# A fused two-block transformer kernel: the first scale and shift computed in eight chunks of 128 features

## The chip, the cores and the metric

The kernel runs on one core of a Trainium2 chip, as one program. The metric is the device time of one execution in microseconds (us); lower is better. TensorE (PE) does the matmuls and the transposes, VectorE (DVE) and ScalarE (ACT) the elementwise work, GpSimd (POOL) a few small operations and the issue of some transfers, and SyncE (SP) issues most transfers. Each engine works through its own instructions strictly in program order; semaphores order the engines against each other.

## The reference, cut to what matters

Two transformer blocks follow each other on x, which has 256 rows (positions) and 1024 features, all in fp32. The change touches the beginning of the first block:

```python
cond = jax.nn.silu(c)
mod = cond @ w_ada[l] + b_ada[l]                 # 1024 x 6144 weight, one row
sh1, sc1, g1, sh2, sc2, g2 = jnp.split(mod, 6, axis=-1)
h = _modulate(x, ln1_g[l], sh1, sc1)             # rms(x, g) * (1 + sc1) + sh1
u = h @ w_in[l]                                  # fox q, k, v | gates | diff q, k, v
fq, fk, fv, fg, dq, dk, dv = jnp.split(u, splits, axis=-1)
...                                              # "fox" attention (8 heads), "diff" attention (4 heads)
x = x + g1[:, None, :] * (mixed @ w_out[l])
```

After that come a gated MLP and a whole second block. They are the same before and after the change.

## The kernel before, in words

**Work list.** A function `plan()` writes one list, ORDER, of steps such as ("piece", ...), ("split", i), ("ada", j), ("evac", T). Each engine walks the whole list and emits only its part of each step. So the order of ORDER is the program order on every engine, and nothing overtakes on an engine.

**Matmuls.** The product is made precise by splitting both operands in two: a weight slab in `raw` (fp32, as loaded) is rounded to `whi` on ACT (L1079) and the rest, raw minus whi, goes to `wlo` on DVE (L1289). This pair is the step `split`. The operand hT has a high and a low half too. One `piece` is one k step (128 features) of one output tile of 256 rows x 512 columns: six matmuls of 512 columns, on the lines L794 (hi x hi), L795 (hi x lo) and L796 (lo x hi), for two row blocks. Output tiles of the first block are fox0 (q), fox1 (k), fox2 (v), diff0, diff1, diff2.

**Buffers.** `raw` has five slots (RAW) and the stream of loads is STREAM: each load waits until the load five places before it has been used. `whi` and `wlo` have three slots (SPL). A split i therefore waits on ACT and on DVE for `gemm_done` to reach i - 2, that is until the last matmul of slab i - 3 is through.

**The start.** `ada` steps multiply w_ada by silu(c), held as 32 equal columns (`cond32`). The first eight of them (L847) make scale and shift of the first norm in two halves of 512 features. A `mod` step brings the result to columns (L868), `turn` steps transpose the normalised x (L904), DVE applies scale and shift (L1388), and `part` steps (L1124 on ACT, L1404 on DVE) split the result into the two halves of hT. Four pieces of fox0 follow with the next four ada steps between them, and then the second half in the same way.

**The way to the first scores.** When a fox tile is complete, `evac` copies it to `tok` (ACT, L1224), squares it to `sq` (ACT, L1229) and sums the squares by head (DVE, L1608). `unit` takes the inverse roots on POOL (L1679 and L1681) and scales tok on DVE (L1450). `heads` transposes q and k of two heads (PE L939) and splits them (ACT L1158 and L1160, DVE L1459 and L1462). `fgate`, `logf` and `cum` make the forget gates: 24 small matmuls (L748), then DVE (L1423, L1425), ACT (an Exp and a Ln with a table load between them), DVE (L1430 to L1436). `vectors`, `setup` and `relbias` prepare small constants on DVE (L1305 to L1329), and POOL issues six transfers for `relbias`. `scores` are the first attention products (L748). After ("scores", 1) the first piece of diff0 follows.

Of the kernel before, what the change touches and what calls it, by code (L numbers as in the profile page):

```python
# [34 lines left out]
P = 128  # L35
# [21 lines left out]
V_C, V_LN1, V_LN2, V_MIX, V_FFN, V_PLE, V_BS, V_QK, V_DN = 0, 8, 16, 24, 32, 40, 48, 56, 60  # L57
V_ALL = 61
# [18 lines left out]
def plan():  # L77
# [81 lines left out]
    def parts(kind, n, pairs):  # L159
# [22 lines left out]
    tail += insert(fill, *[(j, [ada[10 + j]]) for j in range(8)])  # L182
    order += attention(list(range(FOX_P + DIFF_P)), tail, ada[18:20] + [("grow", 0)])
# [79 lines left out]
STREAM = [it for it in ORDER if it[0] in ("split", "ada")]  # L263
# [55 lines left out]
def build(nc, A, out):  # L319

    ctx = ExitStack()
    with ctx:
# [23 lines left out]
        cond32 = sb("cond32", [P, KC, 32])  # L346
        lam = sb("lam", [P, 6])
# [16 lines left out]
        aff1 = sb("aff1", [P, 4, S], F32, gg)  # L364
# [1462 lines left out]
```

## Time and profile before

| | before |
|---|---|
| median of 3 runs | 846.1 us (844.94 to 847.69) |
| profiled execution, span | 845.9 us |
| PE busy | 799.9 us (95%) |
| DVE busy | 473.1 us (56%) |
| ACT busy | 396.7 us (47%) |
| POOL busy | 57.9 us (7%) |
| bytes moved by DMA | 157.87 MB, mean 187 GB/s |

The span runs from the first to the last instruction of the profiled execution; nothing else of that execution's time is shown, and the span stands 0.2 us beside the median. A busy share is the time in which an engine executes, divided by the span. PE is the engine whose work fills the span, so what counts is where it stands idle and where it runs slowly.

### The profile page before, as it was taken

The page shows a single profiled execution, that of the slowest core. Times are in us where ns is not written, and L with a number is a line of the kernel's source. Part 1 is how long each engine was busy: PE and PEld are TensorE (multiplying, and loading weights), DVE is VectorE, ACT ScalarE, POOL GpSimd, SP SyncE. Part 2 cuts the span into 40 slices and gives each one's busy share as a digit, 9 for nine tenths or more (in the row PEclk, how much of TensorE's full clock was granted, in tenths as well). Part 3 has the DMA queues.
Part 4 walks back from the last instruction along what each step waited for, and adds up shares of the span by engine and source line. Part 5 has one row for each costly group of instructions (what it writes and reads, how often), then busy time and mean ns, then how long its engine had stood idle before and what let it go on. Part 6 is the DMA issues. An engine that isn't in the chain of part 4 may idle for free.

```text
span 845.9 us, 10042 instructions
## 1 busy us (share of the span) xinstructions
PE 799.9 (95%) x3874; PEld 628.0 (74%) x3874; DVE 473.1 (56%) x604; ACT 396.7 (47%) x544; POOL 57.9 (7%) x70
## 2 busy tenths in 40 slices
PE   4797999988999999999999999999999999999995
PEld 0266776545788889788878888787888888888884
DVE  0455776556655555553686546556565665535354
ACT  2335665544534444343644347666555454334262
POOL 4013011000000000000252000000000000000001
PEclk9799999999999999999999999999999999999998
DMA  9985245778456537556749564333456465554511
GB/s 292 374 270 188 68 163 196 307 249 313 169 184 199 174 85 239 183 180 198 266 146 333 166 196 149 105 117 117 155 168 199 152 197 159 189 199 143 186 45 50
DMA packets 74128, 157.87 MB, mean 187 GB/s; under 512 B 4046, under 2 KB 6295, under 8 KB 72034
## 3 DMA queue, kind: packets, MB, share of 16 engines
q1 hardware_dynamic: 71072, 151.08, 53.2%
q0 software_dynamic: 1872, 6.11, 2.2%
q8 instruction: 31, 0.51, 0.2%
q10 hardware_dynamic: 1138, 0.06, 0.1%
q14 instruction: 15, 0.12, 0.0%
HBM read 156.16 MB, written 1.07 MB: 186 GB/s over the span
## 4 chain that ended last, share of the span: by engine, by line
PE 87%; ACT 4%; DVE 3%; issue 3%; DMA 2%; SPq 1%; POOL 1%; DVEq 0%; POOLq 0%; ACTq 0%
PE PS L794 25%; PE PS L796 24%; PE PS L795 24%; PE PS L748 3%; PE PS L904 3%; DMA raw<-in_w_ada 2%; PE PS L856 2%; PE PS L847 1%; PE PS L1007 1%; ACT whi L1079 1%; PE PS L977 1%; PE PS L939 1%; SPq L717 1%; DVE wlo L1289 1%; ACT sc L1168 0%
## 5 line engine op out<-in xcount | busy, mean ns | idle before, releaser
L1289 DVE TENSOR_TENSOR wlo<-raw,whi 128x2048 fp32r<-128x2048 f32 (+1 forms) x122 | 279.6, 2294 | 185.1 <-ACT whi L1079 161.0
L1079 ACT ACTIVATE whi<-raw 128x2048 fp32r<-128x2048 f32 (+1 forms) x122 | 226.8, 1859 | 169.7 <-PE PS L796 156.4
L794 PE MATMUL PS<-whi,hT 128*128 128x512 f32 (+1 forms) x704 | 278.3, 395 | 6.4 <-DVE hT L1404 5.9
L796 PE MATMUL PS<-whi,hT 128*128 128x512 f32 (+1 forms) x704 | 272.3, 387 | 0.0
L795 PE MATMUL PS<-wlo,hT 128*128 128x512 f32 (+1 forms) x704 | 271.8, 386 | 0.0
L794 PEld LDWEIGHTS PS<-whi,hT 128*128 128x128 f32 x704 | 132.9, 189 | 36.8 <-issue 8.0
L796 PEld LDWEIGHTS PS<-whi,hT 128*128 128x128 f32 x704 | 132.8, 189 | 27.3
L795 PEld LDWEIGHTS PS<-wlo,hT 128*128 128x128 f32 x704 | 133.1, 189 | 24.3
L794 PE MATMUL PS<-whi,hidT 128*128 128x512 f32 x216 | 86.2, 399 | 0.0
L796 PE MATMUL PS<-whi,hidT 128*128 128x512 f32 x216 | 85.3, 395 | 0.0
L795 PE MATMUL PS<-wlo,hidT 128*128 128x512 f32 x216 | 85.3, 395 | 0.0
L795 PEld LDWEIGHTS PS<-wlo,hidT 128*128 128x128 f32 x216 | 40.6, 188 | 9.8 <-issue 0.2
L796 PEld LDWEIGHTS PS<-whi,hidT 128*128 128x128 f32 x216 | 40.6, 188 | 9.8
L794 PEld LDWEIGHTS PS<-whi,hidT 128*128 128x128 f32 x216 | 40.6, 188 | 9.7 <-issue 0.2
L1168 ACT ACTIVATE sc<-sc,nmax 128x128 f32<-128x128 f32 x64 | 28.6, 449 | 34.6 <-DVE nmax L1501 34.2
L1724 POOL TENSOR_TENSOR nss<-nss 128x2 f32<-128x2 f32 x5 | 0.9, 190 | 589.4 <-ACT mod L1069 361.0
L1129 ACT ACTIVATE hidT<-PS 128x512 fp32r<-128x512 f32 x27 | 14.6, 597 | 43.3 <-PE PS L904 43.3
L748 PEld LDWEIGHTS PS<-kT,qT 128*128 128x128 f32 x192 | 24.6, 190 | 9.0 <-issue 4.4
L748 PE MATMUL PS<-kT,qT 128*128 128x128 f32 (+1 forms) x192 | 27.3, 281 | 3.9 <-DVE kT L1462 2.5
L1409 DVE SCALAR_TENSOR_TENSOR hidT<-PS,hidT 128x512 fp32r<-128x512 f32 x27 | 17.4, 686 | 22.6 <-ACT hidT L1129 22.6
L847 PE MATMUL PS<-raw,cond 128*32 128x512 f32 x64 | 21.6, 813 | 8.7 <-DMA raw<-in_w_ada 8.7
L847 PEld LDWEIGHTS PS<-raw,cond 128*32 128x32 f32 x64 | 3.8, 133 | 23.2 <-issue 14.6
(223 smaller groups left out, 663.7 us busy)
## 6 DMA issues: line engine op xcount, KB each, us to landing
raw<-in_w_in SPq DMA_DIRECT2D x40, 1024.0 KB, 5.3
raw<-in_w_ff SPq DMA_DIRECT2D x32, 1024.0 KB, 5.2
raw<-in_w_ada SPq DMA_DIRECT2D x16, 1024.0 KB, 6.6
raw<-in_w_gate SPq DMA_DIRECT2D x10, 1024.0 KB, 5.1
raw<-in_w_up SPq DMA_DIRECT2D x10, 1024.0 KB, 5.1
raw<-in_w_down SPq DMA_DIRECT2D x10, 1024.0 KB, 5.1
raw<-in_w_ada SPq DMA_DIRECT2D x16, 512.0 KB, 10.3
raw<-in_w_out SPq DMA_DIRECT2D x8, 1024.0 KB, 5.1
```

What stands on the lines that cost most here:

```text
L748: last = pe.matmul(out_ap, a, b, start=(n == 0), stop=(n == len(pairs) - 1))
L794: pe.matmul(o, ah, wh, start=(k == 0), stop=False)
L795: pe.matmul(o, ah, wl, start=False, stop=False)
L796: return pe.matmul(o, al, wh, start=False, stop=end)
L847: last = pe.matmul(PS[r:r + 32, 7 - half, :], cond32[:, 2 * k + c, :], raw[:, slot, (2 * c + j) * W:(2 * c + j + 1) * W], start=(k + c == ...
L856: last = pe.matmul(PS[32 * j:32 * j + 32, 7, :], cond32[:, k, :], raw[:, slot, j * W:(j + 1) * W], start=(k == 0), stop=(k == KC - 1))
L904: last = pe.transpose(PS[:, b, o:o + P], src[:, t, c * P:(c + 1) * P], ident)
L1079: act.activation(slab_view(whi, i % SPL, i), slab_view(raw, slot, i), ACT.Copy).then_inc(hi_made, 1)
L1129: act.activation(hi.rearrange("p c s -> p (c s)"), PS[:, b, :], ACT.Copy, scale=1.0 if gain is None else gain).then_inc(turn_hi, 1)
L1168: act.activation(sc[:, n, c0:c1], sc[:, n, c0:c1], ACT.Exp, bias=nmax[:, a, t:t + 1], scale=-1.0, accum_out=lsum[:, a, t:t + 1]).then_inc( ...
L1289: dve.tensor_tensor(slab_view(wlo, i % SPL, i), slab_view(raw, slot, i), whole(slab_view(whi, i % SPL, i)), ALU.subtract).then_inc(lo_made, 1)
L1409: dve.scalar_tensor_tensor(out=lo.rearrange("p c s -> p (c s)"), in0=PS[:, b, :], scalar=1.0 if gain is None else gain, in1=hi.rearrange(" ...
```

## The change

The first scale and shift no longer come in two halves of 512 features but in eight chunks of 128. For each chunk j the kernel loads 1 MB of w_ada (128 scale columns and 128 shift columns of all 1024 rows, in two transfers of 512 KB with runs of 512 bytes), multiplies it (`rows`), copies the row to SBUF on ACT, turns it into columns with two one-column matmuls (`col`), applies it to the transposed x (`xT`) and splits the result (`part0`). Then come the k step j of fox0 and the k step j of fox1, from one slab of w_in of 128 rows x 1024 columns (0.5 MB). x is the first transfer of SP; c, the identity, ln1_g and the two bias rows are issued by ACT. The order of ORDER changes down to ("scores", 1); behind it the steps are the same.

```diff
-    order += [("cond", 0), ("sums", (0, 0)), ("sums", (0, 1)), ("norm", 0)]
-    order += ada[:4] + [("mod", 0), *turns("norm", 0, (0, 1)), ("split", None), *parts("norm", 0, (0, 1))]
     fox = [tile("fox", n, KC, "h") for n in range(2)]
-    order += insert(slab(fox[0], "w_in", 0, 0), *[(1 + j, [ada[4 + j]]) for j in range(4)])
-    order += [("mod", 1), *turns("norm", 0, (2, 3)), ("split", None), *parts("norm", 0, (2, 3))]
-    order += slab(fox[1], "w_in", W, 0) + [("vectors", 0), ("setup", 0), ("relbias", 0)]
-    order += slab(fox[0], "w_in", 0, 4) + [("evac", fox[0])]
-    now = slab(fox[1], "w_in", W, 4) + [("evac", fox[1])] + whole("fox", 2, "w_in", 2 * W, "h")
-    order += insert(now, (2, [("unit", 0)]), (2, [("fgate", 0)]), (4, [("logf", 0)]), (6, [("unit", 1)]),
-                    (7, [("cum", 0)]), (9, [("heads", 0)]), (10, [("scores", 0), ("heads", 1)]))
+    def chunk(j):
+        return [("col", j), ("split", None), ("part0", j)]
+    order += [("cond", 0), ("chunk", 0), ("sums0", 0), ("norm", 0), ("rows", 0), ("xT", 0), *chunk(0)]
+    order += [("xT", 1), ("chunk", 1), ("rows", 1)]
+    for j in range(KC):
+        slabs.append(dict(weight="w_in", row=j * P, chunks=1, col=0, cols=2 * W))
+        pair = [("piece", dict(T=fox[n], k=j, slab=j, off=n * W, first=n == 0, last=n == 1)) for n in range(2)]
+        order += [pair[0]] + (chunk(j + 1) if j + 1 < KC else []) + [pair[1]]
+        if j + 2 < KC:
+            order += [("xT", j + 2), ("chunk", j + 2), ("rows", j + 2)]
+    order += [("evac", fox[0]), ("evac", fox[1]), ("vectors", 0), ("setup", 0), ("relbias", 0), ("fgate", 0)]
+    now = whole("fox", 2, "w_in", 2 * W, "h")
+    order += insert(now, (1, [("unit", 0)]), (2, [("logf", 0)]), (4, [("unit", 1)]), (6, [("cum", 0)]), (7, [("heads", 0)]))
...
+    order += [("scores", 0), ("heads", 1)]
     order += attention(list(range(FOX_P + DIFF_P)), tail, ada[18:20] + [("grow", 0)])
...
+                if it[0] == "chunk":
+                    dst = raw[:, n % RAW, :].rearrange("p (k a c) -> p k a c", k=KC, a=2)
+                    for a in range(2):
+                        c = a * D + it[1] * P
+                        sp.dma_start(dst[:, :, a, :], A["w_ada"][0, :, c:c + P].rearrange("(k p) c -> p k c", p=P)
+                                     ).then_inc(raw_in[n % RAW], 16)
...
+                elif kind == "rows":
...
+                    for k in range(KC):
+                        r = 32 * (k % 4)
+                        last = pe.matmul(PS[r:r + 32, b, 0:256], cond32[:, k, :], raw[:, slot, k * 256:(k + 1) * 256],
+                                         start=k < 4, stop=k >= 4)
...
+                elif kind == "col":
+                    b = chunk_bank(i)
+                    dve.wait_ge(col_ps, i + 1)
+                    dve.wait_ge(ab0_made, 1 + i)
+                    dve.tensor_scalar(AB[:, 1, i:i + 1], PS[:, b, S:S + 1], col[:, V_B1 + i:V_B1 + i + 1], None, ALU.add)
+                    dve.scalar_tensor_tensor(out=AB[:, 0, i:i + 1], in0=PS[:, b, S + 1:S + 2],
...
+                    dve.tensor_scalar(aff1[:, i % 2, :], PS[:, b, 0:S], AB[:, 0, i:i + 1], AB[:, 1, i:i + 1],
+                                      ALU.mult, ALU.add).then_inc(aff_made, 1)
```

On ACT, at the place where the operand of the first tiles is split, the program before reads as follows (raw and whi are the weight slab and its high half, hT and aff the operand's high half and its source, tok and sq belong to the evacuation; the brackets list the semaphores that an instruction waits for).

```order
L1113 ACTIVATE xn<-x,nrs 128x1024 [waits norm_rs]
L1079 ACTIVATE whi<-raw 128x2048 [waits raw_in4]
L1124 ACTIVATE hT<-aff 128x512 [waits turn_aff] x2
L1079 ACTIVATE whi<-raw 128x2048 [waits raw_in0] x2
L1124 ACTIVATE hT<-aff 128x512 [waits turn_aff,gemm_done] x2
L1079 ACTIVATE whi<-raw 128x2048 [waits gemm_done,raw_in1]
```

In the changed program ACT has this at the second and third chunk (mod is the copied row of a chunk; L1112, L1122 and L1126 are the lines of the weight split, the row copy and the operand split).

```order
L1126 ACTIVATE hT<-aff 128x256 [waits aff_made]
L1122 ACTIVATE mod<-PS 128x256 [waits col_ps,rows_ps]
L1112 ACTIVATE whi<-raw 128x1024 [waits gemm_done,raw_in1]
L1112 ACTIVATE whi<-raw 128x1024 [waits gemm_done,raw_in2]
L1126 ACTIVATE hT<-aff 128x256 [waits aff_made]
L1122 ACTIVATE mod<-PS 128x256 [waits col_ps,rows_ps]
```

A weight split that waits for `gemm_done` now stands directly ahead of every operand split from the third slab on, and DVE has its halves of both in the same order.

On DVE, the program before has the constants, the fox sums and the gate in this order (hss are the sums of squares, wfgs the gate's weights, relrow the relative bias row, fgt the gate).

```order
L1289 TENSOR_TENSOR wlo<-raw,whi 128x2048 [waits gemm_done,hi_made,raw_in1]
L1305 COPY col<-PS 128x45 [waits vec_ps]
...
L1325 TENSOR_TENSOR wfgs<-wfg,wfgs 128x64 [waits wfg_hi,gate_w_in]
L1329 COPY relrow<-PS 16x384 [waits rel_ps]
L1289 TENSOR_TENSOR wlo<-raw,whi 128x2048 [waits gemm_done,hi_made,raw_in2]
L1608 TENSOR_REDUCE hss<-sq 128x16 [waits sq_in]
L1289 TENSOR_TENSOR wlo<-raw,whi 128x2048 [waits gemm_done,hi_made,raw_in3]
L1423 TENSOR_SCALAR fgt<-PS,bf 8x256 [waits fg_ps]
```

In the changed program the same steps stand on DVE like this (L1336 is the weight split, L1669 the sums, L1484 the gate).

```order
L1669 TENSOR_REDUCE hss<-sq 128x16 [waits sq_in] x2
L1380 COPY col<-PS 128x45 [waits vec_ps]
...
L1400 TENSOR_TENSOR wfgs<-wfg,wfgs 128x64 [waits wfg_hi,gate_w_in]
L1404 COPY relrow<-PS 16x384 [waits rel_ps]
L1484 TENSOR_SCALAR fgt<-PS,bf 8x256 [waits fg_ps]
L1486 SCALAR_TENSOR_TENSOR fgt<-fgt 8x256 [waits fg_abs]
L1336 TENSOR_TENSOR wlo<-raw,whi 128x2048 [waits gemm_done,hi_made,raw_in3]
```

Both sums now stand ahead of the constants, and the constants directly ahead of the gate.

## Rows read from the trace of the kernel before

**Rows 1.** The page: the span and the busy time of PE
```profile
span 845.9 us, 10042 instructions
PE 799.9 (95%) x3874; PEld 628.0 (74%) x3874; DVE 473.1 (56%) x604; ACT 396.7 (47%) x544; POOL 57.9 (7%) x70
```

**Rows 2.** Timeline of PE, start: start us, us, engine, line, what, idle before
```profile
9.10 3.63 PE L847 MATMUL PS<-raw,cond 128*32 128x512 f32 x8 [4.96 <-DMA raw<-in_w_ada]
...
32.17 0.76 PE L794 MATMUL PS<-whi,hT 128*128 128x512 f32 x1 [4.45 <-DVE hT L1404]
...
39.92 1.91 PE L847 MATMUL PS<-raw,cond 128*32 128x512 f32 x8
```

**Rows 3.** Timeline: the last unit, heads 0, scores 0, scores 1, first diff0 piece
```profile
80.72 1.23 DVE L1450 TENSOR_TENSOR tok<-tok,hrs 128x1024 f32<-128x1024 f32 x1 [0.38 <-POOL hrs L1681]
...
82.10 0.80 PE L939 MATMUL PS<-con,tok 128*128 128x128 f32 x4 [4.83 <-DVE tok L1450]
...
86.03 0.55 PE L748 MATMUL PS<-kT,qT 128*128 128x128 f32 x3 [0.58 <-DVE kT L1462]
...
94.49 0.55 PE L748 MATMUL PS<-kT,qT 128*128 128x128 f32 x3 [1.36 <-DVE kT L1462]
...
96.90 0.39 PE L794 MATMUL PS<-whi,hT 128*128 128x512 f32 x1
```

**Rows 4.** Groups by form: weight splits; busy us, mean ns, idle before
```profile
L1079 ACT ACTIVATE whi<-raw 128x2048 fp32r<-128x2048 f32 x114 | 218.3, 1915 | 147.1 <-PE PS L796 133.8 <-DMA raw<-in_w_in 13.0
L1289 DVE TENSOR_TENSOR wlo<-raw,whi 128x1024 fp32r<-128x1024 f32 x8 | 9.8, 1224 | 14.2 <-ACT whi L1079 14.1
L1079 ACT ACTIVATE whi<-raw 128x1024 fp32r<-128x1024 f32 x8 | 8.5, 1061 | 22.6 <-PE PS L796 22.6
```

**Rows 5.** Timeline of PE: first matmuls of two pieces, four pieces apart
```profile
57.39 0.50 PE L794 MATMUL PS<-whi,hT 128*128 128x512 f32 x1
...
62.98 0.39 PE L794 MATMUL PS<-whi,hT 128*128 128x512 f32 x1
```

**Rows 6.** A stretch (last columns: granted clock, DMA share, GB/s), and one issue row
```profile
413.00:414.00 1.00, 1.00 (x6) 0.84 (x5) 1.00 (x4) 0.39 (x1) 0.00 (x0) 1.00 1.00 344
...
ws<-in_w_sgu_spatial POOLq DMA_DIRECT2D x1, 512.0 KB, 5.1
```

**Rows 7.** A stretch, same columns: behind the idle time ahead of 32.17
```profile
32.00:38.00 6.00, 5.83 (x14) 2.38 (x14) 2.83 (x3) 0.00 (x0) 0.00 (x0) 0.50 1.05 381
```

**Rows 8.** Timeline: evacuation of fox0, constants, and the gate's matmuls
```profile
58.06 0.21 DVE L1305 COPY col<-PS 128x45 f32<-128x45 f32 x1
...
59.68 0.23 DVE L1325 TENSOR_TENSOR wfgs<-wfg,wfgs 128x64 fp32r<-128x64 f32 x1
...
63.18 1.03 ACT L1224 ACTIVATE tok<-PS 128x1024 f32<-128x1024 f32 x1 [1.79 <-PE PS L796]
...
65.16 1.22 DVE L1608 TENSOR_REDUCE hss<-sq 128x16 f32<-128x1024 f32 x1 [1.39 <-ACT sq L1229]
...
65.70 2.92 PE L748 MATMUL PS<-hT,wfgs 128*8 128x256 f32 x24
```

**Rows 9.** Timeline of POOL: first transfer of relbias, and one inverse root
```profile
60.66 0.59 POOL L1706 DMA_DIRECT2D skew_dram<-relrow  x1 [40.07 <-DVE relrow L1329]
...
66.77 2.94 POOL L1681 TENSOR_TENSOR hrs<-hrs,expo 128x16 f32<-128x16 f32 x1
```

**Rows 10.** Timeline of DVE and ACT: the gate, heads 0, a split
```profile
69.65 0.47 DVE L1423 TENSOR_SCALAR fgt<-PS,bf 8x256 f32<-8x256 f32 x1
...
72.78 0.41 DVE L1430 SCALAR_TENSOR_TENSOR fgt<-fgt 8x256 f32<-8x256 f32 x1 [1.08 <-ACT fgt L1142]
...
74.39 0.41 DVE L1436 SCALAR_TENSOR_TENSOR ncum<-fgt,ncum 8x256 fp32r<-8x256 f32 x1 [0.48 <-ACT ncum L1147]
...
82.93 0.96 ACT L1158 ACTIVATE qT<-PS,col 64x256 fp32r<-64x256 f32 x2 [4.97 <-PE PS L939]
...
86.27 2.29 DVE L1289 TENSOR_TENSOR wlo<-raw,whi 128x2048 fp32r<-128x2048 f32 x1 [0.29 <-issue]
```

More of the change, by code:

```diff
@@ L261 @@
 LAST_SLAB = {p["T"]: p["slab"] for kind, p in ORDER if kind == "piece"}
-STREAM = [it for it in ORDER if it[0] in ("split", "ada")]
+STREAM = [it for it in ORDER if it[0] in ("split", "ada", "chunk")]
 STREAM_AT = {it: n for n, it in enumerate(STREAM)}
 def transfers(it):
-    return 2 if it[0] == "ada" and it[1] < KC else 1
+    return 2 if it[0] == "chunk" else 1
 def spread(ap, n):
@@ L764, in operand_ready @@
                     tn = TILES[T]["name"]
-                    key = {"fox": ("norm", 0), "diff": ("norm", 0), "gate": ("norm", 1), "up": ("norm", 1),
+                    key = {"gate": ("norm", 1), "up": ("norm", 1),
                            "w_out2": ("merge",), "ff1": ("norm", 3), "ple": ("norm", 4)}.get(tn, ("norm", 2))
@@ L815, in _ @@
                 elif kind == "cond":
-                    pe.wait_ge(cond_in, 48)
-                    pe.transpose(PS[:, 5, 0:2 * KC], vec[0:2 * KC, :], ident[0:2 * KC, 0:2 * KC]).then_inc(c_ps, 1)
+                    pe.wait_ge(cond_in, 64)
+                    pe.transpose(PS[:, 5, 0:V_EARLY], vec[0:V_EARLY, :], ident[0:V_EARLY, 0:V_EARLY]).then_inc(c_ps, 1)
                     reader[5] = [(c_col, 1)]
+                elif kind == "rows":
+                    if i == 0:
+                        pe.wait_ge(cond_made, 1)
+                    slot = landed(pe, ("chunk", i))
+                    b = 4 + i % 2
+                    take(b)
+                    for k in range(KC):
+                        r = 32 * (k % 4)
+                        last = pe.matmul(PS[r:r + 32, b, 0:256], cond32[:, k, :], raw[:, slot, k * 256:(k + 1) * 256],
+                                         start=k < 4, stop=k >= 4)
+                    last.then_inc(rows_ps, 1)
+                    reader[b] = [(row_in, i + 1)]
+                elif kind == "xT":
+                    b = chunk_bank(i)
+                    take(b)
+                    pe.wait_ge(xn_act, 1)
+                    pe.wait_ge(xn_dve, 1)
+                    for t in range(TB):
+                        pe.transpose(PS[:, b, t * P:(t + 1) * P], xn1[:, t, i * P:(i + 1) * P], ident)
+                    reader[b] = [(aff_made, i + 1)]
+                elif kind == "col":
+                    pe.wait_ge(row_in, i + 1)
+                    if i == 0:
+                        pe.wait_ge(sel_made, 1)
+                    for a in range(2):
+                        last = pe.matmul(PS[:, chunk_bank(i), S + a:S + a + 1], row_of(i)[:, a * P:(a + 1) * P], sel[:, :],
+                                         start=True, stop=True)
+                    last.then_inc(col_ps, 1)
                 elif kind == "vectors":
@@ L860, in _ @@
-                    last.then_inc(ada_used, 1)
-                elif kind == "mod" and i < 2:
-                    pe.wait_ge(mod_in, i + 1)
-                    take(7 - i)
-                    r = slice(64 * i, 64 * i + 64)
-                    for c in range(4):
-                        last = pe.transpose(PS[:, 7 - i, c * 64:(c + 1) * 64], mod[r, 0, c * P:(c + 1) * P], ident[r, r])
-                    last.then_inc(mod_T, 1)
-                    reader[7 - i] = [(ab_made, 1 + i)]
+                    if k == 0:
+                        take(7)
@@ L872, in _ @@
+                    for j in range(4):
+                        last = pe.matmul(PS[32 * j:32 * j + 32, 7, :], cond32[:, k, :],
+                                         raw[:, slot, j * W:(j + 1) * W], start=(k == 0), stop=(k == KC - 1))
+                    if k == KC - 1:
+                        reader[7] = [(mod_in, pack)]
+                    last.then_inc(ada_used, 1)
                 elif kind == "mod":
                     for n, pk in enumerate((1, 2)):
-                        pe.wait_ge(mod_in, pk + 2)
+                        pe.wait_ge(mod_in, pk)
@@ L910, in _ @@
                     pe.wait_ge(wfg_lo, 1)
-                    pe.wait_ge(turn_lo, TURNS[("norm", 0, 3)] + 1)
+                    pe.wait_ge(part_lo, KC)
                     pe.wait_ge(wfg_hi, 1)
```

183 lines of the change are left out of this document (91 added, 92 removed).

## The prediction

> **What bounds the kernel now.** I read the page first: PE is busy for 799.9 us of the 845.9 us span [rows 1], so a change pays only where PE stands idle or runs slowly. The timeline of PE then shows the first 97 us as the place where both happen. The first ada matmuls start at 9.10 us, when their weights land, and the first piece only at 32.17 us [rows 2]. There is a second hole of 4.83 us ahead of heads 0 at 82.10, and one of 1.36 us ahead of scores 1 at 94.49. The first diff0 piece follows at 96.90 [rows 3]. Behind it both programs have the same steps in the same order, so I forecast when the changed program reaches this piece, and carry the shift to the end. The profiled execution (span 845.9) stands 0.2 us from the median, so the shift can be added to either.
>
> **First part, to the first pair.** x comes first and chunk 0 behind it, so 2 MB must land, not 1 MB as at 9.10. At the 381 GB/s that the transfers reach in a full stretch [rows 7], 1 MB takes 2.7 us; less what no longer precedes it (b_ada), I put chunk 0 at 10.5, and slab 0 and chunk 1 (1.5 MB) at 14.6. In the meantime come the norm, the first transposes and col 0. Rows 1 takes half of what two ada steps (eight logical matmuls, 3.63 us for x8 records at the low clock) took per column, 1.7 us here. The first pair starts at about 17.5: 14.7 us earlier than now. L847 also gets cheaper: eight matmuls of 256 columns in four column groups, against four of 512 in two groups, which took 1.91 us at the high clock [rows 2]; I take 0.9 us. This is what the change gives.
>
> **Second part, the eight pairs.** Here I expect the loss. A piece is (62.98 - 57.39)/4 = 1.40 us [rows 5]. The order shown for ACT has, from the third slab on, a weight split that waits for gemm_done ahead of the operand split. Followed through the list: between fox0 k(j) and fox1 k(j) stand col(j+1), split(j+3), part0(j+1); `whi` has three slots, so split j+3 waits for slab j, whose last matmul is the end of fox1 k(j). And fox0 k(j+1) needs part0(j+1). So PE must finish the pair, then wait for the split on ACT (1.06 us), the split on DVE (1.22 us, both 128x1024 [rows 4]) and DVE's operand half. That last one and the hops I estimate at 0.5 us, from the 0.4 us that instructions of 8x256 take [rows 10]. The period is two pieces 2.8 + col 0.25 (no row shows its two one-column matmuls; they cost between nothing and the 0.78 us of two 512-column records [rows 5], and I take 0.25, nearer nothing since they stream one column) + 1.06 + 1.22 + 0.5 = 5.85 us. PE's own further work in it, rows 0.9 and xT 0.3, lies under the 2.8 us of waiting and costs nothing; without that cover it would be 1.2 us a pair. The first period has no such wait and takes 5.1. Slabs 8 and 9 are full 128x2048 slabs (1.92 us on ACT, 2.29 us on DVE [rows 4, 10]), and part0 6 and part0 7 stand behind their splits: two periods of 5.85 + 0.86 + 1.07 = 7.8 us. Sum: 17.5 + 5.1 + 4 x 5.85 + 2 x 7.8 + 2.9 for the last pair = 64.5 us.
>
> **The clock in it.** In the last two periods PE waits for 3.7 and 4.8 us. After the idle time ahead of 32.17 the clock stood at 0.50, the 1.2 GHz level, for all of 32 to 38 us [rows 7], and after the 4.83 us ahead of 82.10 pieces ran at half pace too. If the last two pairs run at the low clock they cost up to 2.8 us more each. I take 3.5 of these 5.6: fox1 ends at 68.
>
> **Third part, from there to diff0.** Both fox tiles complete together, and the order for DVE shows both sums, then the constants, then the gate. Step by step, from the end of fox1:
> - ACT copies and squares fox0 (0.93 to the start of the square, then 1.05, as 63.18 to 65.16 [rows 8]) and DVE sums (1.22): 3.2. The second square waits for that sum, since `sq` is one buffer: 1.0 + 1.22: 5.5.
> - Constants on DVE, 58.06 to 59.91: 1.85 [rows 8]: 7.4. Only now are the gate's weights there. PE has 1 us of work until then and idles some 6.4 us; queued behind its gate matmuls are all pieces of fox2. So these 2.75 us (65.70 to the next piece) come at the low clock, 5.5: 12.9.
> - DVE and ACT on the gate, 69.65 to 72.78: 3.1 [rows 10]; then split 10 stands in both queues, 1.92 and 2.29: 20.2. (POOL meanwhile issues relbias's six transfers at 0.59 each and two inverse roots of 3.2 each [rows 9]: done by 17.9, hidden by this; without it they would be the last.)
> - unit 0 1.2 [rows 3], the rest of the gate 72.78 to 74.80, 2.0, unit 1 1.2: 24.6. The eight fox2 pieces (11.2 us) lie beside this.
> - heads 0 on PE 0.5; ACT's part 1.45; DVE's split 11 and its part of heads: scores 0 follows the heads transposes by 3.9 us now (82.10 to 86.03 [rows 3, 10]): 29.
> - scores 0 to scores 1 is 8.46 us now [rows 3]. DVE was busy for part of it with a split from 86.27 [rows 10], so 7.3 to 8.5, but now no fox2 piece stands between and PE idles again, 4.5 us. 37.
> - scores 1 takes 2.4 us, or 4.8 at the low clock, and scores 0 may lose 1.5 too: 39.4 to 43.5. I take 42.5, since the hole ahead of scores 1 is as long as that ahead of 82.10.
>
> **The sum.** Diff0 starts at 68 + 42.5 = 110.5 instead of 96.90: 13.6 us later, of which 14.7 is gained at the start and 28.3 lost after it. 845.9 + 13.6 = 859.5; I say **860 us**.
>
> **The price of the short runs.** The chunks come in runs of 512 bytes, which the SP queue did not carry before. The fast end is 381 GB/s [rows 7], 2.7 us a chunk. The nearest rows are of ws, 1024 runs of 512 bytes issued by POOL: 344 GB/s in the stretch 413 to 414, and 5.1 us for 512 KB from issue to landing [rows 6], which is 10.3 us a chunk if nothing overlapped. Since transfers do overlap, I take 344, 3.05 us. With the 1.4 us of a half slab the transfers then need 4.45 us a pair, hidden under the 5.85 us. They decide only from 4.45 us a chunk on, 235 GB/s.
>
> The Trainium skill, "DMA: Bandwidth & Descriptors", section "Anatomy of one DMA — SWDGE (gpsimd) path", gives a transfer 2.0 us plus its bytes at 436 GB/s, an estimate of 3.2 us for 512 KB alone, 6.4 us a chunk if its two did not overlap. By that rule the loads would bound the pairs at 7.8 us and the time would be near the slow-load rival below; by the rows, where the ada transfers had 512 KB too and the queue moved 381 GB/s, they stay hidden. The row decides.
>
> **The rivals.**
> - *The chunks load slowly.* At 6 to 6.4 us a chunk a pair takes 7.4 to 7.8 us, and all eight 59 to 62 from 17.5 or later; fox1 ends near 79, diff0 starts near 121: **870 us**. For it: no row shows the SP queue with such runs. Against it: the 344 GB/s. Chance 0.15.
> - *The clock stays high* in the last pairs and at the scores: 64.5 + 39.4 = 103.9, **853 us**. Against it: both holes that long before 32.17 and 82.10 were followed by the low level. Chance 0.12.
> - *Faster: the splits do not hold the operand.* If the weight split ran ahead of the pair, a period would be PE's own 2.8 + 0.25 + 0.9 + 0.3 = 4.25 or the loads' 4.45. Fox1 then ends at 17.5 + 7 x 4.45 + 2.9 = 51.6, diff0 starts at 51.6 + 39.4 = 91, and the time is **840 us**. It decides where the mean period is below 5.2 us (17.5 + 7 x 5.2 + 2.9 + 39.4 = 96.2). For it: 14.7 us are really gained at the start. Against it: the brackets in the order and the three slots. Chance 0.06.
> - *The change moves the start, and the loss is just the gain,* 846 us: 0.04.
>
> **The numbers.** The forecast as told has 0.63, its own range being 854 to 867. The range of 8 in 10 reaches from the high-clock rival to the slow loads, 852 to 872. A run can tell about 0.3% (2.5 us) from no change. Faster by more than that: 0.06; within it: 0.04; slower: 0.90.
>
> **What would show it.** The first piece starts at 16 to 19 us; the pairs of fox0 and fox1 repeat every 5.6 to 6.2 us with PE waiting some 1.6 us for DVE's operand half, and 7.5 us or more in the last two; whi for slab j+3 starts on ACT right at the end of fox1 k(j); fox1 ends at 64 to 70; the gate's matmuls wait 6 us or more for wfgs; scores 1 waits over 4 us; diff0 starts at 104 to 113. The forecast is wrong if a pair takes less than 5.2 us, if rows waits for raw at every chunk (slow loads), or if the shift at diff0 is not the shift at the end.

## The result, and the profile after

The changed kernel takes 868.67 us (median of 4 runs, 867.91 to 870.78) against 845.52 us (843.99 to 847.69) before: the ratio is 1.0272, with a 95% interval from 1.0246 to 1.0297. The forecast was 860 with 852 to 872 as the range of 8 in 10. So the direction and that range held, but not the narrower 854 to 867 that the forecast as told gave itself, and the shift of 23.1 us was forecast as 14.

The page after shows PE busy for as long as before [rows 1], in a longer span:

```profile
span 867.4 us, 10280 instructions
...
PE 801.0 (92%) x3962; PEld 638.7 (74%) x3962; DVE 476.6 (55%) x626; ACT 398.1 (46%) x554; POOL 56.0 (6%) x65
```

The timeline of PE says where the 21.5 us of span went. In brackets stands the idle time before an instruction and what ended it. L816 at these places is the first matmul of fox0's k step of a chunk, L768 the gate and then the scores, and the last row is the first diff0 piece, which answers to the last of [rows 3].

```profile
19.86 1.94 PE L851 MATMUL PS<-raw,cond 128*32 128x256 f32 x16
21.98 0.76 PE L816 MATMUL PS<-whi,hT 128*128 128x512 f32 x1 [0.18 <-DVE hT L1375]
...
33.40 0.47 PE L816 MATMUL PS<-whi,hT 128*128 128x512 f32 x1 [1.73 <-DVE hT L1375]
...
39.82 0.47 PE L816 MATMUL PS<-whi,hT 128*128 128x512 f32 x1 [1.73 <-DVE hT L1375]
...
61.00 0.77 PE L816 MATMUL PS<-whi,hT 128*128 128x512 f32 x1 [3.65 <-DVE hT L1375]
...
72.09 0.77 PE L816 MATMUL PS<-whi,hT 128*128 128x512 f32 x1 [4.87 <-DVE hT L1375]
...
84.80 4.13 PE L768 MATMUL PS<-hT,wfgs 128*8 128x256 f32 x24 [6.54 <-DVE wfgs L1400]
...
104.59 0.55 PE L768 MATMUL PS<-kT,qT 128*128 128x128 f32 x3 [1.97 <-DVE kT L1523]
...
112.10 0.90 PE L768 MATMUL PS<-kT,qT 128*128 128x128 f32 x3 [4.53 <-DVE kT L1523]
...
116.54 0.63 PE L816 MATMUL PS<-whi,hT 128*128 128x512 f32 x1
```

The first pair starts 10.2 us earlier than the first piece did [rows 2]. The second pair follows at 26.98 without a wait. From the third on PE stands before every pair and waits for DVE's operand half, with a period of 6.42 us, then 8.34 and 11.09. Diff0 begins at 116.54 in place of 96.90: 19.6 us of the 21.5 are lost by then, and the last 1.9 later.

The engines' timeline inside one period shows why PE waits 1.73 us. ACT's split (L1112) starts right after the pair's last matmul, DVE's split (L1336) follows, and only then the operand half (L1375) for which PE stands:

```profile
34.86 0.50 PE L871 MATMUL PS<-sel,mod 128*128 128x1 f32 x4
...
35.78 0.54 DVE L1369 TENSOR_SCALAR aff<-PS,AB 128x256 f32<-128x256 f32 x1
36.71 0.38 PE L862 MATMUL PS<-con,xn 128*128 128x128 f32 x2
36.97 1.06 ACT L1112 ACTIVATE whi<-raw 128x1024 fp32r<-128x1024 f32 x1 [4.79 <-PE PS L818]
37.02 1.07 PE L851 MATMUL PS<-raw,cond 128*32 128x256 f32 x16
37.93 0.40 ACT L1126 ACTIVATE hT<-aff 128x256 fp32r<-128x256 f32 x1
38.12 1.23 DVE L1336 TENSOR_TENSOR wlo<-raw,whi 128x1024 fp32r<-128x1024 f32 x1 [1.79 <-ACT whi L1112]
38.24 0.36 ACT L1122 ACTIVATE mod<-PS 128x256 f32<-128x256 f32 x1
39.26 0.42 DVE L1375 TENSOR_TENSOR hT<-aff,hT 128x256 fp32r<-128x256 f32 x1
```

`aff` was ready at 36.3 and its two halves need 0.8 us, so PE could have had its operand at 37.2. But ACT was idle until 36.97, in a wait for the pair to end (PE PS L818), with the operand split queued behind. The small step stood behind the large one in both queues.

Stretches (columns as in [rows 6]) show the clock: behind the wait of 1.73 us it is 1.00 (first row), and behind the long waits PE is at the low level for the whole of each stretch; full speed comes back later.

```profile
33.00:34.00 1.00, 0.60 (x3) 0.55 (x4) 0.25 (x1) 0.00 (x0) 0.00 (x0) 1.00 1.18 297
61.00:67.00 6.00, 6.00 (x16) 4.63 (x16) 0.89 (x3) 0.00 (x0) 0.00 (x0) 0.50 0.89 313
71.00:77.00 6.00, 4.91 (x12) 3.93 (x13) 0.94 (x2) 0.00 (x0) 0.00 (x0) 0.50 0.52 175
...
112.00:116.00 4.00, 3.90 (x18) 3.90 (x19) 1.24 (x7) 0.44 (x3) 0.00 (x0) 0.50 0.00 0
```

### The profile page after: what moved, and what is told of

Same layout as the page of the kernel before. It is cut to its first block, busy times and chain, and to the rows that moved or that the text cites. A ratio compares the mean times of both kernels' runs of the same rounds, so it can differ in the third digit from the quotient of the medians.

```text
span 867.4 us, 10280 instructions
## 1 busy us (share of the span) xinstructions
PE 801.0 (92%) x3962; PEld 638.7 (74%) x3962; DVE 476.6 (55%) x626; ACT 398.1 (46%) x554; POOL 56.0 (6%) x65
## 3 DMA queue, kind: packets, MB, share of 16 engines
q0 software_dynamic: 1744, 5.85, 2.3%
HBM read 155.90 MB, written 1.07 MB: 181 GB/s over the span
## 4 chain that ended last, share of the span: by engine, by line
PE 79%; ACT 3%; DVE 2%; issue 2%; POOL 0%; DVEq 0%; POOLq 0%; ACTq 0%
PE PS L816 23%; PE PS L818 23%; PE PS L817 23%; PE PS L768 3%; PE PS L934 2%; PE PS L896 1%; PE PS L1037 1%; PE PS L1007 1%; ACT whi L1112 1%; PE PS L969 1%; ACT sc L1215 1%; PE PS L919 0%; ACT pt L1224 0%; PE PS L1068 0%; PE PS L1038 0%
## 5 line engine op out<-in xcount | busy, mean ns | idle before, releaser
L1336 DVE TENSOR_TENSOR wlo<-raw,whi 128x2048 fp32r<-128x2048 f32 (+1 forms) x126 | 280.3, 2226 | 204.9 <-ACT whi L1112 179.9
L1112 ACT ACTIVATE whi<-raw 128x2048 fp32r<-128x2048 f32 (+1 forms) x126 | 227.4, 1805 | 189.0 <-PE PS L818 188.7
L816 PE MATMUL PS<-whi,hT 128*128 128x512 f32 (+1 forms) x704 | 281.5, 400 | 17.0 <-DVE hT L1375 15.6
L818 PE MATMUL PS<-whi,hT 128*128 128x512 f32 (+1 forms) x704 | 274.2, 390 | 0.0
L816 PEld LDWEIGHTS PS<-whi,hT 128*128 128x128 f32 x704 | 134.3, 191 | 47.8 <-issue 23.7
L818 PEld LDWEIGHTS PS<-whi,hT 128*128 128x128 f32 x704 | 134.1, 191 | 27.8
L816 PE MATMUL PS<-whi,hidT 128*128 128x512 f32 x216 | 86.1, 398 | 0.0
L818 PE MATMUL PS<-whi,hidT 128*128 128x512 f32 x216 | 85.2, 394 | 0.0
L816 PEld LDWEIGHTS PS<-whi,hidT 128*128 128x128 f32 x216 | 40.6, 188 | 9.9 <-issue 0.2
L818 PEld LDWEIGHTS PS<-whi,hidT 128*128 128x128 f32 x216 | 40.5, 188 | 9.8
L768 PE MATMUL PS<-kT,qT 128*128 128x128 f32 (+1 forms) x192 | 28.6, 290 | 8.5 <-DVE kT L1523 7.1
L768 PEld LDWEIGHTS PS<-kT,qT 128*128 128x128 f32 x192 | 25.9, 199 | 13.1 <-DVE kT L1523 8.0
L1176 ACT ACTIVATE hidT<-PS 128x512 fp32r<-128x512 f32 x27 | 14.6, 597 | 43.4 <-PE PS L934 43.4
L1301 ACT ACTIVATE hid<-PS 128x1024 f32<-128x1024 f32 x8 | 8.2, 1027 | 24.1 <-PE PS L818 24.1
L1224 ACT ACTIVATE pt<-PS 128x384 f32<-128x384 f32 x28 | 13.5, 485 | 9.6 <-PE PS L1007 9.6
```

Of the source, the lines that this page charges most:

```text
L768: last = pe.matmul(out_ap, a, b, start=(n == 0), stop=(n == len(pairs) - 1))
L816: pe.matmul(o, ah, wh, start=(k == 0), stop=False)
L818: return pe.matmul(o, al, wh, start=False, stop=end)
L1112: act.activation(slab_view(whi, i % SPL, i), slab_view(raw, slot, i), ACT.Copy).then_inc(hi_made, 1)
L1176: act.activation(hi.rearrange("p c s -> p (c s)"), PS[:, b, :], ACT.Copy, scale=1.0 if gain is None else gain).then_inc(turn_hi, 1)
L1224: act.activation(probs_T(u)[:, j % 2, :], PS[:, probs_bank(n), 0:3 * P], ACT.Copy).then_inc(probs_sb, 1)
```

## The experiments

Each ratio is to the kernel before, run on the same chip. "Less" and "more" without another name are against the 868.67 us of the changed kernel. The runs were made in groups (v1 to v4, v5 to v8, v9 to v11, v12), and beside them the kernel before had medians of 846.86, 846.93, 846.25 and 846.27 us, against 845.52 beside the changed kernel. So a difference below 1.5 us between two groups says nothing by itself; there the traces have to speak.

**v1: the weight split behind the operand split.**

```diff
-        return [("col", j), ("split", None), ("part0", j)]
+        return [("col", j), ("part0", j), ("split", None)]
```

> This kernel is the changed one with each weight split of the pair stretch put behind the operand split of the same chunk, so that on ScalarE and VectorE the small step that TensorE waits for no longer stands behind a 1 us weight split. Theory A (the pair stretch is bound by the two weight splits that stand in the chain from the column to the operand): the period of a pair falls from 6.42 us by about the 1.06 us of ScalarE's split, or the 1.23 us of VectorE's, whichever is the longer in the chain, and by the short copies before them, to some 4.8 us, TensorE's clock stays at 1.00 through the last two pairs, the second fox tile ends at about 59 us in place of 77, and the whole takes about 850 us. Theory B (the stretch is bound by the chunk transfers of 512-byte runs, or by the weights for the pairs): the period stays above 6 us, and the whole stays within 3 us of 868.7. Theory C (the weight splits themselves, now later, are what TensorE waits for): the wait moves to the split's low half, and the whole gains less than 8 us.

Measured: 856.02 us, ratio 1.0104 (1.008 to 1.0129), 12.6 us less. The waits for `hT` that stood before every pair are gone but one of 0.51 us, so theory A names the cause. It overstates the gain, for the timeline of PE shows what came next: rows (L851) now wait for their chunk, pair 7 starts at 59.98, 36.6 us behind the first pair at 23.36 (a mean period of 5.23, not 4.8), and the gate's wait is exactly as long as before. The first pair itself now waits 1.39 us for its high half of the weights, whose split stands behind: a small part of theory C.

```profile
23.36 0.77 PE L816 MATMUL PS<-whi,hT 128*128 128x512 f32 x1 [1.39 <-ACT whi L1112]
...
39.12 1.07 PE L851 MATMUL PS<-raw,cond 128*32 128x256 f32 x16 [0.81 <-DMA raw<-in_w_ada]
48.93 1.07 PE L851 MATMUL PS<-raw,cond 128*32 128x256 f32 x16 [0.21 <-DMA raw<-in_w_ada]
54.97 1.07 PE L851 MATMUL PS<-raw,cond 128*32 128x256 f32 x16 [1.31 <-DMA raw<-in_w_ada]
59.98 0.47 PE L816 MATMUL PS<-whi,hT 128*128 128x512 f32 x1 [0.51 <-DVE hT L1375]
70.34 5.25 PE L768 MATMUL PS<-hT,wfgs 128*8 128x256 f32 x24 [6.54 <-DVE wfgs L1400]
```

**v2: the constants behind pair 4.**

```diff
-    order += [("evac", fox[0]), ("evac", fox[1]), ("vectors", 0), ("setup", 0), ("relbias", 0), ("fgate", 0)]
+        if j == 4:
+            order += [("vectors", 0), ("setup", 0), ("relbias", 0)]
+    order += [("evac", fox[0]), ("evac", fox[1]), ("fgate", 0)]
```

> This kernel is the changed one with the constants (vectors, setup, relative-bias row) put behind pair 4 in place of behind the two fox evictions. If the 6.54 us wait ahead of the gate matmuls is VectorE's queue (evictions, then the constants, then the gate's weight split), the gate matmuls start about 1 us after the end of the second fox tile, their wait is under 2 us, they run at the high clock, and the whole takes about 6 us less than 868.7, some 862 to 863 us. If the gate is held by the evictions alone, or the constants now lengthen the pairs by the same amount (they stand on VectorE, which each pair waits for), the whole is within 2 us of 868.7.

Measured: 860.46 us, ratio 1.016 (1.0138 to 1.0182), 8.2 us less. In the timeline of PE the gate follows the fox tiles without a wait and at the high clock; pair 6 and pair 7 wait as long as before, so VectorE had room for the constants.

```profile
61.88 0.76 PE L818 MATMUL PS<-whi,hT 128*128 128x512 f32 x1 [3.65 <-DVE hT L1377]
71.61 0.62 PE L818 MATMUL PS<-whi,hT 128*128 128x512 f32 x1 [4.87 <-DVE hT L1377]
76.03 2.90 PE L770 MATMUL PS<-hT,wfgs 128*8 128x256 f32 x24
```

**v3: v1 and v2 together.**

> Both edits together: the weight splits behind the operand splits, and the constants behind pair 4. If the two waits are separate they add: 18 us and 6 us off 868.7, some 845 us, within half a per cent of the kernel before the change. If the first edit already gives the VectorE time back that the second needs (the constants then fall in a stretch where VectorE has no room), the whole is above 850 us.

Measured: 849.6 us, ratio 1.0029 (1.0017 to 1.0041), 19.1 us less. The single gains sum to 20.9, so they nearly add. It stays above 845 mostly because v1's gain was less than expected. For the 1.8 us that are missing from the sum no cause is shown; 1.1 us of it stand at the start, where v3's first pair came at 24.49 and v1's at 23.36, in a stretch in which the two kernels have the same steps.

**v4: v3 with the four small loads first.**

```diff
+            sp.dma_start(vec[V_C:V_C + KC, :], A["c"].rearrange("a (r q) -> (a r) q", q=P)).then_inc(cond_in, 16)
...
             sp.dma_start(x[:, :, :], A["x"][0].rearrange("(t p) d -> p t d", p=P)).then_inc(x_in, 16)
...
-            act.dma_start(vec[V_C:V_C + KC, :], A["c"].rearrange("a (r q) -> (a r) q", q=P)).then_inc(cond_in, 16)
```

> The kernel with both edits, and the four small loads that the conditioning needs (c, the identity, ln1_g, b_ada) issued by SyncE ahead of x in place of by ScalarE. If the late first pair (21.98 us against the 17.5 forecast) comes of these loads landing at 10.3 us behind the bulk of x, and of ScalarE's transfer issues that hold up its square until 14.6 us, the conditioning's transpose runs some 6 us earlier, the first pair starts at 18 us or before, and the whole takes 3 to 4 us less than the kernel with both edits. If the start is bound by x and the first weights (x's own landing, then the norm), the first pair moves by under 1 us, and x, now behind four loads, may land later by up to that.

Measured: 847.9 us, ratio 1.0013 (0.9998 to 1.0028), 1.7 us less than v3 where 3 to 4 were expected. The first pair starts at 21.92 in place of 24.49, not at 18. Its period is steady at 4.88 us (rows at 37.05, 41.93, 46.81), and PE is busy for nearly all of it.

```profile
20.06 1.94 PE L858 MATMUL PS<-raw,cond 128*32 128x256 f32 x16 [1.58 <-DMA raw<-in_w_ada]
21.92 0.80 PE L823 MATMUL PS<-whi,hT 128*128 128x512 f32 x1
...
37.05 1.07 PE L858 MATMUL PS<-raw,cond 128*32 128x256 f32 x16 [0.17 <-DMA raw<-in_w_ada]
41.93 1.07 PE L858 MATMUL PS<-raw,cond 128*32 128x256 f32 x16 [0.16 <-DMA raw<-in_w_ada]
46.81 1.07 PE L858 MATMUL PS<-raw,cond 128*32 128x256 f32 x16 [0.18 <-DMA raw<-in_w_ada]
```

**v9: the same loads first, alone on the changed kernel.**

> This kernel is the changed one with one edit: the four small loads of the conditioning go ahead of x on SyncE's queue. Theory A (the late first pair is the matter of these loads and of ScalarE's queue behind them): the first pair starts at 18 us and the whole takes some 3.5 us less. Theory B, from the trace of the kernel with three edits: the first norm and column come 1.5 us earlier, but TensorE's order has the rows of chunk 1 ahead of the first pair, and they waited there for their transfer until 20.06 us and took 1.94 us; then the first pair starts at 22.0 us as before and the whole stays within 1 us of 868.7.

Measured: 867.28 us, ratio 1.0246 (1.0224 to 1.0267), 1.4 us less. In total that is within what two groups differ by, but the trace bears it out, for its first pair starts at 20.59 in place of 21.98. Theory B has the mechanism, and its size was off by these 1.4 us: the conditioning's transpose runs at 5.89 in place of 10.34 and the operand's low half is there at 19.1, but rows 1, which stands ahead of the pair in PE's order, waits for chunk 1 until 18.72. The pair starts when it ends.

```profile
5.89 0.31 PE L844 MATMUL PS<-con,vec 32*128 32x32 f32 x1 [5.89 <-DMA vec<-in_b_ada]
...
18.66 0.42 DVE L1375 TENSOR_TENSOR hT<-aff,hT 128x256 fp32r<-128x256 f32 x1
18.72 1.93 PE L856 MATMUL PS<-raw,cond 128*32 128x256 f32 x16 [1.54 <-DMA raw<-in_w_ada]
20.59 0.80 PE L821 MATMUL PS<-whi,hT 128*128 128x512 f32 x1
```

**v7 and v8: chunks in 4 KB rows,** on the changed kernel and on v1.

```diff
-                        c = a * D + it[1] * P
-                        sp.dma_start(dst[:, :, a, :], A["w_ada"][0, :, c:c + P].rearrange("(k p) c -> p k c", p=P)
+                        sp.dma_start(raw[:, n % RAW, a * D:(a + 1) * D],
+                                     A["w_ada"][0, it[1] * P:(it[1] + 1) * P, a * D:(a + 1) * D]
```

> This kernel is the changed one with each chunk's two transfers read as 128 rows of 4 KB in place of 1024 rows of 512 bytes: the same bytes into the same slot, but not the features that the reference wants, so scale and shift of the first norm come out of the wrong weights. Theory A (the pairs are bound by the two engines that split, and the transfers are hidden): the period stays at 6.42 us and the whole within 2 us of 868.7. Theory B (the 512-byte runs slow what the queue brings): the period falls below 6 us and the whole by more than 4 us.

> The kernel with the splits behind the operand split (856.0 us), and the chunks read in 4 KB rows as in the run before this (wrong weights for the first norm). In its own trace the rows of the chunks waited 0.2 to 1.3 us for their transfer, at a DMA share of 1.10. If the short runs had become its limit, these waits go, the period falls towards the 4.7 us that TensorE's own work of a pair takes, and the whole takes 2 to 5 us less; if the waits are those of bytes and not of runs, the whole stays within 1.5 us of 856.

Measured: v7 868.96 us, ratio 1.0259 (1.0236 to 1.0281), no change: theory A, the loads are hidden in the changed kernel. The queue did become faster: from 12 to 18 us it moved 403 GB/s in v7 and 331 in the changed kernel, and the period stayed at 6.43 us. v8 854.43 us, ratio 1.0092 (1.0062 to 1.0122), 1.6 us less than v1, with intervals that overlap: it lies between its two bounds and settles little. It does say that the short runs are not the main thing that held v1 above 850, since the rows still waited for chunks twice (0.72 and 0.47 us).

**v6 and v10: products of no use in PE's holes,** to keep the clock.

```diff
+        order += {6: [("warm", (4, 14))], 7: [("warm", (4, 19))]}.get(j, [])
         order += [pair[0]] + (chunk(j + 1) if j + 1 < KC else []) + [pair[1]]
...
-    order += [("evac", fox[0]), ("evac", fox[1]), ("vectors", 0), ("setup", 0), ("relbias", 0), ("fgate", 0)]
+    order += [("evac", fox[0]), ("evac", fox[1]), ("vectors", 0), ("setup", 0), ("relbias", 0), ("warm", (7, 26)), ("fgate", 0)]
...
-    order += [("scores", 0), ("heads", 1)]
+    order += [("scores", 0), ("heads", 1), ("warm", (7, 16))]
...
+                    for _ in range(n):
+                        pe.matmul(PS[:, b, :], hT[:, 0, 0, 0:P], hT[:, 0, 0:2, :], start=True, stop=True)
```

This is v10; v6 had bank 4 for the 26 ahead of the gate.

> This kernel is the changed one with products of no use added on TensorE: 14 of 512 columns ahead of pair 6, 19 ahead of pair 7, 26 ahead of the gate and 16 ahead of scores 1, into banks that nothing else holds then; at the high clock they take 3.2, 4.3, 5.9 and 3.6 us, each less than the wait that stands there (3.65, 4.87, 6.54, 4.53 us). The output is as before. If the holes cost their own length alone, the whole stays at 868.7. If a hole also costs the half clock of the stretch behind it (pair 6 took 5.97 us of matmuls for 3.3, pair 7 5.2 for 2.8, the gate 4.1 for 2.8, scores 1 4.4 for 2.4), the granted clock stays at 1.00 from 55 us to the third part and the whole takes 6 to 9 us less, some 861 us.

Measured for v6: 867.18 us, ratio 1.0242 (1.022 to 1.0263), 1.5 us less. The pairs did keep the clock, but the 26 products waited 5.20 us for the constants that had bank 4, ran for 8.10 us and held up the gate, so the total says nothing on the theory.

> The kernel with the added products again (14, 19, 26 and 16 of 512 columns, output as before), those ahead of the gate now in a bank of which they need not wait for the constants; in the first try they waited 5.20 us there, ran 8.10 us at the low clock and put the gate off by 3 us, so that the price of the low clock was not measured past pair 7. Theory A (a hole costs also the low clock of what follows it): as pair 6 to pair 7 took 8.35 us in place of 11.09 there, and with the gate at 3 us in place of 4.1 and scores 1 at 2.4 in place of 4.4, the whole takes some 5 us less than 868.7. Theory B (the low clock of a stretch is hidden, since the next wait there is for the two splitting engines): the whole takes 2 us less or nothing.

Measured for v10: 862.6 us, ratio 1.0189 (1.0167 to 1.0211), 6.1 us less, theory A. The same three waits and the gate in its timeline of PE, now short, with pair 6 to pair 7 in 8.35 us in place of 11.09:

```profile
62.35 0.47 PE L817 MATMUL PS<-whi,hT 128*128 128x512 f32 x1 [0.25 <-DVE hT L1382]
70.70 0.47 PE L817 MATMUL PS<-whi,hT 128*128 128x512 f32 x1 [0.55 <-DVE hT L1382]
81.04 2.97 PE L769 MATMUL PS<-hT,wfgs 128*8 128x256 f32 x24 [0.43 <-DVE wfgs L1407]
...
108.67 0.55 PE L769 MATMUL PS<-kT,qT 128*128 128x128 f32 x3 [0.75 <-DVE kT L1530]
```

PE worked more (810.8 us busy against 801.0) and ended sooner: some 6 us of the loss are the clock behind the holes, over and above the holes. The traces agree: from pair 6 to diff0 it is 48.7 us here (62.35 to 111.06) and 55.5 in the changed kernel (61.00 to 116.54), and that although scores 0 ran at the low clock here (3.9 us in place of 2.4).

**v5 and v11: the waits behind the fox tiles.** v5 is v4 with the cumulative gate ahead of the next weight split and four diff0 pieces around scores 0 and heads 1. v11 is v5 with unit 0 moved ahead of that split as well (the cut is against the changed kernel):

```diff
-    order += insert(now, (1, [("unit", 0)]), (2, [("logf", 0)]), (4, [("unit", 1)]), (6, [("cum", 0)]), (7, [("heads", 0)]))
+    order += insert(now, (0, [("unit", 0), ("logf", 0)]), (4, [("unit", 1), ("cum", 0)]), (6, [("heads", 0)]))
...
-    order += [("scores", 0), ("heads", 1)]
-    order += attention(list(range(FOX_P + DIFF_P)), tail, ada[18:20] + [("grow", 0)])
+    order += tail[:1] + [("scores", 0), ("heads", 1)] + tail[1:4]
+    order += attention(list(range(FOX_P + DIFF_P)), tail[4:], ada[18:20] + [("grow", 0)])
```

In return the fill behind scores 1, around the softmax of unit 0, has four pieces fewer; v12 below has the same.

> The kernel with the three edits (split behind operand, constants early, conditioning loads first), and a fourth: VectorE and ScalarE do the cumulative forget gate ahead of the next weight split, and four pieces of the first diff tile stand around scores 0 and heads 1 in place of behind scores 1. In the trace without it TensorE waits 4.08 us for fgt, 1.43 us for kT ahead of scores 0 and 4.52 us for kT ahead of scores 1, which then run at half the clock. If these waits are only a matter of what stands behind them in TensorE's order, the first and the last go, and with the clock kept at 1.00 through scores 1 the whole takes 8 to 11 us less than 847.9, some 838 us, faster than the kernel before the change. If the pieces' weights are not split by then (VectorE has two 2.29 us splits in this stretch), the wait moves to the low half and the whole stays within 2 us of 847.9.

Measured for v5: 845.65 us, ratio 0.9992 (0.9977 to 1.0008), 2.3 us less than v4. The waits shrank from 4.08, 1.43 and 4.52 us to 1.60, none and 2.91, but a new one of 2.33 us for `tok` stood ahead of heads 0: neither theory.

> The kernel with four edits (845.65 us), and the first head scaling put ahead of the next weight split on VectorE: in its trace TensorE waits 2.33 us for tok ahead of heads 0, and VectorE does a 2.29 us split before the 1.2 us scaling. If that wait is VectorE's order alone, it goes, the clock stays at 1.00 from 70 to 90 us (it was 0.83 there), and the whole takes 2 to 4 us less, some 842.5 us and faster than the kernel before the change by 0.4 per cent. If the head's scaling is bound by the inverse root on GpSimd (2.9 us, ended at 72 us), or if the later weight split becomes what the pieces wait for, it stays within 1 us of 845.65.

Measured for v11: 843.36 us, ratio 0.997 (0.9957 to 0.9983), 2.3 us less than v5: the wait for `tok` fell to 0.97. The clock was not 1.00 from 70 to 90 us, as expected, but 0.91, and 2.98 us of waiting for `kT` stayed ahead of scores 1. This is the fastest version, and it beats the kernel before by 0.3%, about the least that a run can tell.

```profile
71.41 0.26 PE L963 MATMUL PS<-con,fgt 8*128 8x8 f32 x2 [1.60 <-DVE fgt L1495]
77.17 0.63 PE L976 MATMUL PS<-con,tok 128*128 128x128 f32 x4 [0.97 <-DVE tok L1513]
```

**v12: the same filling on the kernel before,** to see whose gain that is.

```diff
-                    (7, [("cum", 0)]), (9, [("heads", 0)]), (10, [("scores", 0), ("heads", 1)]))
+                    (7, [("cum", 0)]), (13, [("heads", 0)]))
...
+    order += tail[:1] + [("scores", 0), ("heads", 1)] + tail[1:4]
```

> This kernel is the one before the change, with only the last idea of the best version so far: heads 0 behind all eight pieces of the third fox tile in place of behind four, and four pieces of the first diff tile around scores 0 and heads 1. It tells whose gain the 0.3 per cent of that version is. Theory A (the filled holes would help either design): TensorE's waits of 4.83 us ahead of heads 0 and 1.36 us ahead of scores 1 go, with the low clock behind the first, and the whole takes 3 to 6 us less than the kernel before, as fast as the best version of the chunked design or faster. Theory B (moving heads 0 back makes the attention chain behind it later, where VectorE's next splits stand): the wait returns ahead of scores 0 or 1, and the whole stays within 1.5 us of the kernel before.

Measured: 845.75 us, ratio 0.999 (0.9975 to 1.0005): theory B. The 4.83 us ahead of heads 0 [rows 3] are gone, and these came in their place in its timeline of PE (the second was followed by the low clock). So the filling alone does not bring the 0.3% of v11. But the intervals of the two overlap, and whether the chunked start brings it is not shown.

```profile
86.53 0.55 PE L749 MATMUL PS<-kT,qT 128*128 128x128 f32 x3 [1.75 <-DVE kT L1463]
95.89 0.55 PE L749 MATMUL PS<-kT,qT 128*128 128x128 f32 x3 [2.22 <-DVE kT L1463]
```

## Why the prediction was right, and where its sizes were off

**The mechanism** was that of the forecast: an early start, then a chain pair, ACT split, DVE split, operand half. The pattern in the trace is as foretold, v1 shows by its one edit that the order is the cause of 12.6 us, v2 that the constants ahead of the gate are that of 8.2 us, and v7 that the loads are not. The slow-load rival falls with v7, the high-clock rival with the stretches at 0.50, and the faster rival needed the splits out of the way, which the change did not do.

The sizes were worse than the total looks. Of the signs named, the chain, the 6.54 us ahead of the gate and the 4.53 us ahead of scores 1 came. But the first piece (21.98, put at 16 to 19), the period (6.42, put at 5.6 to 6.2), fox1's end (77.29, put at 64 to 70) and diff0 (116.54, put at 104 to 113) all came behind their ranges, and the shift at diff0 was not that at the end. That the total stayed near was partly luck, since the third part was put too long. And by the time alone 868.67 lies nearer the slow-load rival's 870 than the forecast's 860; only the trace and v7 tell them apart.

**First part: 17.5, measured 21.98,** 4.5 us too early. The step reckoned x and the weights, not the four small loads. ACT issued them within 3 us, yet the transpose that needs them ran at 10.34 us; ACT then issued eleven more transfers from 10.92 to 14.54 ahead of its square. (The Trainium skill, "DMA: Bandwidth & Descriptors", section "Issuing engines are not separate DMA queues", says that issuing from a second engine saves only the time to issue. By that rule the small loads share the DMA engines with x and the first chunk, and the traces agree: the transpose ran at 10.34 us with them on ACT beside x, and at 5.89 in v9, where they go first.) v9 also shows the next bound, chunk 1, which I put at 14.6 us and which landed at 18.7. So of the 4.5 us, v9 gives back 1.4, and the rest is chunk 1 and its rows, which stand ahead of the pair and take 1.94 us here against 1.07 in the later pairs. How much of chunk 1's 4.1 us the short runs cost is open, for no run has 4 KB rows and the small loads first together.

**Second part: 50.5 us from first pair to the end of fox1, measured 55.3.** The period was put at 5.85 and is 6.42. By the rows of the one period above it is 3.31 us for the two pieces and the column (33.40 to 36.71; 3.05 forecast), 1.06 and 1.23 for the two splits (1.06 and 1.22 forecast) and 0.82 for the rest, DVE's operand half and all hops, which I had put at 0.5: the half alone takes 0.42, and 0.26 pass from the pair's end to ACT's split. So about half of the 0.57 is pieces and column and half is hops. Over the four periods with this chain that is 2.3 us; the first took 5.0 against 5.1. The last two, forecast at 7.8, were 8.34 at the high clock and 11.09 at the low. For **the clock** I had allowed 3.5 us. It took 11.09 - 8.35 = 2.7 us in pair 6 (against v10) and 5.2 us in place of 2.8 in pair 7 (against v6, 71.28 to 74.10, and v10, 70.70 to 73.52), 5.1 together.

**Third part: 42.5, measured 39.2.** The gate started 7.5 us after fox1's end, as forecast at 7.4, and its wait of 6.54 us was as told. But the clock came back within the gate's matmuls, so that the next piece followed 4.0 us behind their start (84.80 to 88.77) and not 5.5. That is most of the 1.7 us by which scores 0 came earlier than told. From there to scores 1 it was 7.5 us and not 8, and scores 1 took 4.4 us at the low clock, where I had 5.5 for it and a part of scores 0's low clock; scores 0 ran at the high clock. (The upper end of that step adds up to 43.3 and not 43.5, which changed nothing.)

**The sum** was short by 4.5 + 4.8 - 3.3 = 6.0 us at diff0 (a shift of 19.6 against 13.6), and 1.9 us are lost behind diff0; the forecast had carried the shift to the end unchanged. In the timelines of PE they stand in one place, 117 us behind diff0, where both kernels have the same steps. L934 and L904 are the transposes of a later norm's result, and the pieces follow them. This is the changed kernel:

```profile
229.62 2.52 PE L934 MATMUL PS<-con,xnb 128*128 128x128 f32 x16 [2.05 <-ACT xnb L1160]
233.05 0.77 PE L816 MATMUL PS<-whi,hT 128*128 128x512 f32 x1 [0.90 <-DVE hT L1465]
...
237.78 0.40 PE L818 MATMUL PS<-whi,hT 128*128 128x512 f32 x1
```

And this the kernel before:

```profile
210.18 1.94 PE L904 MATMUL PS<-con,xnb 128*128 128x128 f32 x16 [2.06 <-ACT xnb L1113]
213.60 0.47 PE L794 MATMUL PS<-whi,hT 128*128 128x512 f32 x1 [1.49 <-DVE hT L1404]
...
216.22 0.39 PE L796 MATMUL PS<-whi,hT 128*128 128x512 f32 x1
```

The first and the twelfth matmul behind the transposes are shown: the shift is 19.45 us at the first and 21.56 at the twelfth, and so it stays to the end. The granted clock was 0.50 from 233 to 237 us, and 1.00 from 214 to 217 before, behind waits of nearly the same length. Among the traces of the other versions v1 and v12 have this low stretch (0.50 and 0.52) and the rest do not, so it looks like a matter of the single execution and not of the change; that is not shown.

**The base** was off as well. A profiled execution takes 1.8 us more than its span (869.17 us for 867.4), so that by the same difference the span of before [rows 1] belongs to an execution of 847.7 us, 2.2 above its median of 845.52, not 0.2 below. I had compared a span with a time. All together: 859.5 + 6.0 + 1.9 + 1.8 = 869.2, the profiled execution, with the median of four 0.5 below it.

**The assumption on the clock** held for the long waits: in the changed kernel the granted clock was 1.00 behind the four waits of 1.73 us and 0.50 behind those of 3.65, 4.87 and 4.53 us. Between them it went either way: the 1.97 us ahead of scores 0 were followed by the low level in v10 and not in the changed kernel, and the 2.05 and 0.90 us ahead of 233.05 by the low level there, while 2.06 and 1.49 us at the same place before were not.

## What to carry to other kernels

When work is cut into more and smaller steps, look at what each step stands behind in every in-order queue: a 0.4 us operand split behind two 1 us weight splits cost 12.6 us over the eight chunks, and swapping two entries of the work list gave it back. A hole on PE costs its own length and then the clock behind it, here 6 us over four holes, so price the stretch after a wait too. Once one bound goes, the next stands close (chunk transfers, then PE's own 4.7 us a pair, for which the fast rival had 4.25), so take the single gains as upper limits; and compare a span only with a span.

## What the runs showed of the hardware

- Small loads issued by ACT by 2.9 us were there for PE only at 10.3 us, with x and the first chunk issued by SP beside them. With all on SP and the small ones first, it was 5.9 us in v9 and 7.9 us in v4, though the two queues begin alike.
- The SP queue with 512-byte runs moved 297 GB/s at a DMA share of 1.18 (33 to 34 us), against 381 at 1.05 with longer runs [rows 7]. At the same place, from 12 to 18 us, it was 331 GB/s at 1.12 in the changed kernel and 403 at 1.03 in v7 with 4 KB rows. It cost nothing there, since it was hidden.
- With the added products of v10 PE was busy for 9.8 us longer, and the kernel ended 6.1 us sooner.
